# A head's value weights hold its high and low parts side by side: two matmul passes per key tile instead of three, and one VectorE addition per head

## The chip, the core and the metric

One core of a Trainium2 chip runs the whole kernel. The metric is the time of one execution on the device, in microseconds (us), lower is better. The engines are TensorE (PE: matmuls; PEld: its weight loads), VectorE (DVE), ScalarE (ACT), GpSimd (POOL) and SyncE (SP, which here only issues the weight transfers). Each has its own instruction stream; they meet at semaphores.

## What is computed

A two-layer decoder trunk on 512 positions of width 1024, in float32. What matters here are its attention heads of width 64:

```python
# layer B: 12 heads of forgetting attention over the 512 positions (causal)
sc = q @ k.T * scale + logcum_q - logcum_k ; p = softmax(where(mask, sc, -inf)) ; out = p @ v
# layers A and B: 4 heads each of attention into 256 memory tokens
p = softmax(qm @ mk.T * scale) ; out = p @ mv
# then y = concat(mix, mo) @ w_o, layer norms, squared-ReLU MLP
```

Around them stand layer A's gated mixer (a projection, a layer norm, a 128x128 spatial gate), the output projections and the two MLPs.

## The kernel before

Every float32 factor of a matmul is split into a high part (rounded to the reduced float32 type F32R) and a low part (what is left), and a product is three passes: high x high, high x low, low x high. `products` (line 428) issues such passes; nearly all rows of matmuls have its line, L431. `project` (line 439) multiplies a 128-column block of weights by a 128 x 8 x 512 operand: 8 blocks of k, 3 passes each. The weights come by DMA into `w_raw`; ScalarE rounds them to `w_hi` (L844), VectorE subtracts to `w_lo` (L1203, the line of every such subtraction, `rest`), and TensorE waits for that.

Attention goes by steps of two heads (`pair_step`, written out on each engine: lines 551, 916, 1317). Steps 0 and 1 are the memory heads of layer A, 2 (STEP_B) and 9 (STEP_LAST) those of layer B, 3 to 8 the six pairs of fox heads. A step has eight units u, four query blocks for each head. For a unit, TensorE makes the scores (`scores`, bank `sc`), VectorE the row maximum (`row_max`, L1250), ScalarE the exponential (L888), VectorE the normalisation (`normalize`, L1258, tile `probs`), TensorE turns the result (`turn`, L462, bank `tr`), ScalarE takes the high part (`turned_probs`, tiles `pb_hi` for fox, `pa_hi` and `pm_hi` for memory) and VectorE the low part (`pb_lo`, `pa_lo`, `pm_lo`). Then `attend(s, head)` (line 521) multiplies the value weights with them into the bank `pv[head]`. A value tile has 128 columns, 64 of each head of the pair, so that 128 rows come out, of which only the head's own 64 are read. A fox head has four key tiles and sees 512, 384, 256 and 128 queries in them (12 matmuls), a memory head two tiles of 512 (6 matmuls). ScalarE copies the own rows to `mix_hi` (L899) and VectorE subtracts to `mix_lo` (`attended`, line 1266), which raises `mix_ready`.

The order is written by hand. TensorE: for u = 0 to 7 a piece of a projection (`filler(u)`), `turn(u - 2)`, `scores(u)`; then `attend(s, 0)`, `turn(6)`, `filler(8)`, `turn(7)`, `filler(9)`, `attend(s, 1)`, and in steps 2 to 7 `turn_values` (L548), which turns the next pair's values. `attend(s, 1)` waits for the low part of unit 7. VectorE's queue after the last unit: low part of unit 6, `attended(0)`, low part of unit 7, `w_lo` of the next block, a key part, the two `cum_rows` (L1313), `attended(1)`, and the values' low part `v_lo`; then the next step's first `row_max`. Steps 0 to 7 have a projection to put between the units; step 8 and STEP_LAST have only pieces of the output projection (`out_start`), and the last pieces of it need `mix_ready` of the last head. Behind STEP_B, VectorE works on the cumulated gates (`cum`) before `cum_rows`; behind step 1 it begins the spatial gate (L1561).

Of the kernel before, what the change touches and what calls it, by code (L numbers as in the profile page):

```python
# [21 lines left out]
F32 = mybir.dt.float32  # L22
F32R = mybir.dt.float32r

P = 128
HALF = P // 2
# [37 lines left out]
def trunk_kernel(nc, x, mem, a_w_in, a_sgu_ln_g, a_sgu_ln_b, a_w_s, a_b_s, kv_w, kv_b_f, b_w_q,  # L64
# [4 lines left out]
    TT = T // P  # L69
# [40 lines left out]
    with ctx:  # L110
# [3 lines left out]
        def sem(name):  # L114
            return ctx.enter_context(nc.semaphore(name))
# [4 lines left out]
        def put(name, shape, dtype, offset=None):  # L120
            size = 4
            for n in shape[1:]:
                size *= n
            if offset is None:
                offset = base[0]
                base[0] += (size + 63) // 64 * 64
            assert offset + size <= nc.sbuf_usable_end, (name, offset + size)
            return nc.alloc_sbuf_tensor_at(name, shape, dtype, offset=offset)
# [8 lines left out]
        w_raw = put("w_raw", [P, 2, KT, P], F32)  # L137
        mk_twice = put("mk_twice", [P, 2 * MEMPAIRS, M], F32R)
        mk_rest = put("mk_rest", [P, 2 * MEMPAIRS, M], F32R)
        mv_hi = put("mv_hi", [P, MT, MEMPAIRS * P], F32R)  # L140
        mv_lo = put("mv_lo", [P, MT, MEMPAIRS * P], F32R)
        ident = put("ident", [P, P], F32)
        ident_r = put("ident_r", [P, P], F32R)
        ones_r = put("ones_r", [P, P], F32R)
# [51 lines left out]
        qc = put("qc", [P, 2, 2, T], F32R, A0 + 8 * K1)  # L196
        ks = put("ks", [P, 2, 2, T], F32R, A0 + 16 * K1)
        kc = put("kc", [P, 2, 2, T], F32R, A0 + 24 * K1)
        v_hi = put("v_hi", [P, 2, TT, P], F32R, A0 + 32 * K1)
        v_lo = put("v_lo", [P, 2, TT, P], F32R, A0 + 36 * K1)  # L200
        B0 = A0 + 40 * K1

        pb_hi = [put("pb_hi0", [P, TT + 1, T], F32R, B0), put("pb_hi1", [P, TT, TT + 1, P], F32R, B0)]
# [75 lines left out]
        sc_done, max_done, exp_done = sem("sc_done"), sem("max_done"), sem("exp_done")  # L279
        inv_done, probs_ready = sem("inv_done"), sem("probs_ready")  # L280
        pv_done, mix_hi_ready, mix_ready = sem("pv_done"), sem("mix_hi_ready"), sem("mix_ready")
        vt_done, vt_hi, vt_ready = sem("vt_done"), sem("vt_hi"), sem("vt_ready")
        row_ready = sem("row_ready")
        wf_hi_ready, wf_ready = sem("wf_hi_ready"), sem("wf_ready")
# [33 lines left out]
        def fox(s):  # L318
            return STEP_FOX <= s.base < STEP_LAST
# [16 lines left out]
        def other_rows(head):  # L336
            return own_rows(1 - head)
# [89 lines left out]
        def _(pe):  # L427
            def products(target, terms, start=True, stop=True):

                for n, (lhs, rhs) in enumerate(terms):  # L430
                    last = pe.matmul(target, lhs, rhs, start=start and n == 0,  # L431
                                     stop=stop and n == len(terms) - 1)
                return last
# [87 lines left out]
            def attend(s, head):  # L521

                pe.wait_ge(tr_free, tr_index(s, head * TT + TT - 1).at(1))
                wait(pe, mix_ready, s.at(head - 1, 2))
                if s.base == STEP_B and head == 1:
                    pe.wait_ge(f_step, 1)
                c = step_kind(s).slot
                if fox(s) and head == 0:
                    pe.wait_ge(vt_ready, step_kind(s).at(1))
                tiles = TT if fox(s) else MT  # L530
                for j in range(tiles):
                    seen = slice(j * P if fox(s) else 0, T)
                    if fox(s):
                        vh, vl = v_hi[:, c, j], v_lo[:, c, j]
                    else:
                        vh, vl = mv_hi[:, j, c * P:(c + 1) * P], mv_lo[:, j, c * P:(c + 1) * P]
                    ph, pl = seen_places(s, head, j)
                    last = products(pv[head][:, seen], [(vh, ph), (vh, pl), (vl, ph)], j == 0, j == tiles - 1)
                last.then_inc(pv_done, 1)

            def turn_values(s, j):
# [295 lines left out]
        def _(act):  # L837
# [8 lines left out]
            def turned_hi(t, target, source=None):  # L846

                act.wait_ge(tr_done, t.at(1))
                act.copy(target, tr[t.slot][:, :] if source is None else source).then_inc(tr_hi, 1)
# [30 lines left out]
                halves(b, g, [qm[own_rows(head), 2 * c + head, :] for head in range(2)], scale=SCALE)  # L880

            def memory_values(layer):
                turned_hi(Pos(T_MV[layer]), mv_hi[:, :, :], tr[T_MV[layer] % 2][:, :].rearrange("p (m c) -> p m c", m=MT))

            def exponentials(s, u):
                n = keys(s, u) * P
# [29 lines left out]
            def pair_step(s, b=None, g=None, values=None, late=None):  # L916

                mixing = b is not None and s.base < STEP_B
                reading = b is not None and s.base >= STEP_B
                for u in range(8):  # L920
                    if mixing and u in (0, 3, 6):
                        prepare(b.plus(u // 3 + 1))
                    if reading and u in (0, 4, 7):
                        prepare(b.plus((u + 2) // 3 + (u == 0)))
                    if late is not None and u == 1:
                        prepare(late)
                    if u >= 2:
                        turned_probs(s, u - 2)
                    exponentials(s, u)
                    if mixing and u in (2, 5):  # L930
                        step_projection(s, b.plus(u // 3), g.plus(u // 3), u // 3)
                    if reading and u == 2:
                        for head in range(2):
                            fox_head(b, g, 0, head)
                    if reading and u in (5, 6):
                        fox_head(b.plus(1), g.plus(1), 1, u - 5)
                attended(s, 0)
                turned_probs(s, 6)
                turned_probs(s, 7)
                if b is not None:  # L940
                    step_projection(s, b.plus(2), g.plus(2), 2)
                attended(s, 1)
                if values is not None:
                    act.wait_ge(vt_done, values.at(1))
                    act.copy(v_hi[:, values.slot], pv[0][:, :].rearrange("p (t c) -> p t c", t=TT)).then_inc(vt_hi, 1)

            def squares(n, j, g):

# [251 lines left out]
        def _(dve):  # L1200
            def rest(target, whole, hi):

                return dve.tensor_tensor(target, whole, hi.bitcast(F32), ALU.subtract)  # L1203
# [8 lines left out]
            def turned_lo(t, h, target, hi, source=None):  # L1212

                dve.wait_ge(tr_hi, h.at(1))
                rest(target, tr[t.slot][:, :] if source is None else source, hi).then_inc(tr_free, 1)
# [26 lines left out]
                       [qm[own_rows(head), 2 * c + head, :] for head in range(2)], SCALE)  # L1242

            def memory_values(layer):
                turned_lo(Pos(T_MV[layer]), Pos(H_MV[layer]), mv_lo[:, :, :], mv_hi[:, :, :],
                          tr[T_MV[layer] % 2][:, :].rearrange("p (m c) -> p m c", m=MT))

            def row_max(s, u):
                dve.wait_ge(sc_done, s.at(u + 1, 8))
# [16 lines left out]
            def attended(s, head):  # L1266
                rows = slice(head * HALF, (head + 1) * HALF)
                tile = bass.ds(step_tile(s), 1)
                dve.wait_ge(mix_hi_ready, s.at(head + 1, 2))
                rest(mix_lo[rows, tile, :], pv[head][rows, :].rearrange("p (a t) -> p a t", a=1),  # L1270
                     mix_hi[rows, tile, :]).then_inc(mix_ready, 1)

            def gate_stats(n):

# [42 lines left out]
            def pair_step(s, b=None, g=None, values=None, late=None):  # L1317
                mixing = b is not None and s.base < STEP_B
                reading = b is not None and s.base >= STEP_B
                for u in range(8):  # L1320
                    row_max(s, u)
                    if mixing and u in (0, 3, 6):
                        prepare(b.plus(u // 3 + 1))
                    if reading and u in (0, 4):
                        prepare(b.plus(u // 4 + 1))
                    if late is not None and u == 1:
                        prepare(late)
                    if u >= 2:
                        turned_probs(s, u - 2)
                    normalize(s, u)  # L1330
                    if s.base == STEP_A and 1 <= u <= TT:
                        gate_norm(u - 1)
                    if reading and u in (2, 3):
                        fox_query(values, g, u - 2)
                    if reading and u == 6:
                        fox_key(values, g.plus(1), 0)
                turned_probs(s, 6)
                attended(s, 0)
                turned_probs(s, 7)
                if reading:  # L1340
                    prepare(b.plus(3))
                    fox_key(values, g.plus(1), 1)
                if fox(s) and values is not None:
                    cum_rows(values)
                attended(s, 1)
                if values is not None:
                    dve.wait_ge(vt_hi, values.at(1))
                    rest(v_lo[:, values.slot], pv[0][:, :].rearrange("p (t c) -> p t c", t=TT),
                         v_hi[:, values.slot]).then_inc(vt_ready, 1)

            def residual(n, b, g, j, first=True, target=None):

# [447 lines left out]
```

## Time and profile before

| | us |
|---|---|
| median of 3 runs | 1239.83 |
| lowest and highest run | 1237.76, 1242.72 |
| span of the profiled execution | 1237.6 |
| TensorE busy in it | 1162.2 |
| VectorE busy | 649.8 |
| ScalarE busy | 482.1 |

The profile shows one execution; its span runs from the first to the last instruction. Matmuls are pipelined and overlap in the rows, so that their spacing is read from their starts and not from their durations. Some instructions are merged on one row (x2, x12). A bracket such as [0.47 <-ACT mix_hi L899] says how long the engine sat idle before that instruction, and which instruction released it.

### The profile page before, as it was taken

The page shows a single profiled execution, that of the slowest core. Times are in us where ns is not written, and L with a number is a line of the kernel's source. Part 1 is how long each engine was busy: PE and PEld are TensorE (multiplying, and loading weights), DVE is VectorE, ACT ScalarE, POOL GpSimd, SP SyncE. Part 2 cuts the span into 40 slices and gives each one's busy share as a digit, 9 for nine tenths or more (in the row PEclk, how much of TensorE's full clock was granted, in tenths as well). Part 3 has the DMA queues.
Part 4 walks back from the last instruction along what each step waited for, and adds up shares of the span by engine and source line. Part 5 has one row for each costly group of instructions (what it writes and reads, how often), then busy time and mean ns, then how long its engine had stood idle before and what let it go on. Part 6 is the DMA issues. An engine that isn't in the chain of part 4 may idle for free.

```text
span 1237.6 us, 15886 instructions
## 1 busy us (share of the span) xinstructions
PE 1162.2 (94%) x5444; PEld 957.3 (77%) x5444; DVE 649.8 (53%) x1000; ACT 482.1 (39%) x805; POOL 158.5 (13%) x141
## 2 busy tenths in 40 slices
PE   6997989899999999999989999798999999999994
PEld 5776768688888888788668888676788888888883
DVE  4457776654323444343577777667544323544325
ACT  4334633644212334222655556434533222442221
POOL 2204144300000000021501000034200000000002
PEclk9998999899999999999899999998999999999997
DMA  7521132233333333333212121113233333333221
GB/s 215 141 69 51 51 103 83 62 94 102 102 92 95 98 89 102 102 88 92 60 52 69 52 68 52 35 56 98 85 98 90 102 102 87 101 102 101 87 85 68
DMA packets 200714, 107.48 MB, mean 87 GB/s; under 512 B 4512, under 2 KB 197344, under 8 KB 200672
## 3 DMA queue, kind: packets, MB, share of 16 engines
q1 hardware_dynamic: 194304, 99.10, 28.1%
q10 hardware_dynamic: 6368, 7.82, 2.1%
q8 instruction: 26, 0.43, 0.2%
q14 instruction: 16, 0.13, 0.0%
HBM read 104.81 MB, written 2.10 MB: 86 GB/s over the span
## 4 chain that ended last, share of the span: by engine, by line
PE 82%; DVE 10%; ACT 5%; issue 2%; DMA 1%; DVEq 0%; ACTq 0%
PE proj L431 75%; PE pv L431 3%; DVE w_lo L1203 2%; PE tr L462 2%; PE sc L431 2%; ACT w_hi L844 1%; ACT probs L888 1%; DVE probs L1258 1%; DVE neg_max L1250 1%; PE sc L655 1%; DVE mix_lo L1203 1%; DMA w_raw<-in_mem_w_kv 1%; DVE y_nat L1633 0%; DVE z_nat L1288 0%; DVE y_nat L1647 0%
## 5 line engine op out<-in xcount | busy, mean ns | idle before, releaser
L1203 DVE TENSOR_TENSOR w_lo<-w_raw,w_hi 128x1024 fp32r<-128x1024 f32 x186 | 245.7, 1321 | 170.4 <-ACT w_hi L844 167.4
L431 PE MATMUL proj<-x_hi,w_hi 128*128 128x512 f32 x784 | 314.6, 401 | 11.7 <-ACT x_hi L976 6.0
L431 PE MATMUL proj<-x_hi,w_lo 128*128 128x512 f32 x784 | 309.3, 394 | 0.0
L431 PE MATMUL proj<-x_lo,w_hi 128*128 128x512 f32 x784 | 309.0, 394 | 0.0
L844 ACT CAST w_hi<-w_raw 128x1024 fp32r<-128x1024 f32 x186 | 194.3, 1045 | 261.9 <-PE proj L431 259.2
L431 PE MATMUL proj<-h_hi,w_hi 128*128 128x512 f32 x512 | 200.1, 391 | 0.8 <-DVE w_lo L1203 0.8
L431 PE MATMUL proj<-h_hi,w_lo 128*128 128x512 f32 x512 | 199.3, 389 | 0.0
L431 PE MATMUL proj<-h_lo,w_hi 128*128 128x512 f32 x512 | 199.2, 389 | 0.0
L431 PEld LDWEIGHTS proj<-x_hi,w_hi 128*128 128x128 f32 x784 | 149.1, 190 | 45.7 <-ACT x_hi L976 10.4
L431 PEld LDWEIGHTS proj<-x_hi,w_lo 128*128 128x128 f32 x784 | 149.3, 190 | 31.1
L431 PEld LDWEIGHTS proj<-x_lo,w_hi 128*128 128x128 f32 x784 | 149.5, 191 | 29.4 <-POOL x_lo L1668 0.7
L1435 DVE TENSOR_TENSOR h_raw<-relu 128x512 f32<-128x512 f32 x64 | 44.3, 692 | 153.6 <-ACT relu L865 153.6
L865 ACT ACTIVATE relu<-proj 128x512 f32<-128x512 f32 x64 | 38.3, 598 | 192.1 <-PE proj L431 192.1
L431 PEld LDWEIGHTS proj<-h_hi,w_hi 128*128 128x128 f32 x512 | 96.1, 188 | 20.9 <-DVE w_lo L1203 1.2
L431 PEld LDWEIGHTS proj<-h_hi,w_lo 128*128 128x128 f32 x512 | 96.1, 188 | 20.1
L431 PEld LDWEIGHTS proj<-h_lo,w_hi 128*128 128x128 f32 x512 | 96.1, 188 | 19.8
L888 ACT ACTIVATE probs<-sc,neg_max 128x256 f32<-128x256 f32 (+2 forms) x80 | 40.6, 508 | 69.7 <-DVE neg_max L1250 69.6
L431 PE MATMUL proj<-mix_hi,w_hi 128*128 128x512 f32 x128 | 51.9, 405 | 2.9 <-DVE w_lo L1203 1.7
L1668 POOL TENSOR_TENSOR x_lo<-x,x_hi 128x512 fp32r<-128x512 f32 x32 | 43.6, 1373 | 76.0 <-ACT x L972 46.1
L1203 DVE TENSOR_TENSOR h_lo<-h_raw,h_hi 128x512 f32 (+1 forms) x64 | 44.3, 693 | 15.8 <-ACT h_hi L995 15.5
L462 PE MATMUL tr<-ident,probs 128*128 128x128 f32 x184 | 36.3, 292 | 16.1 <-DVE probs L1258 15.7
L431 PE MATMUL proj<-mix_hi,w_lo 128*128 128x512 f32 x128 | 50.5, 394 | 0.0
(223 smaller groups left out, 1292.1 us busy)
## 6 DMA issues: line engine op xcount, KB each, us to landing
w_raw<-in_w_up SPq DMA_DIRECT2D x64, 512.0 KB, 4.1
w_raw<-in_w_down SPq DMA_DIRECT2D x64, 512.0 KB, 3.8
w_raw<-in_w_o SPq DMA_DIRECT2D x16, 512.0 KB, 3.9
w_raw<-in_a_w_in SPq DMA_DIRECT2D x14, 512.0 KB, 3.8
w_raw<-in_kv_w SPq DMA_DIRECT2D x12, 512.0 KB, 3.8
w_raw<-in_mem_w_kv SPq DMA_DIRECT2D x8, 512.0 KB, 5.9
w_raw<-in_b_w_q SPq DMA_DIRECT2D x8, 512.0 KB, 3.8
x_nat<-in_x ACTq DMA_DIRECT2D x2, 1024.0 KB, 12.4
```

The costliest lines, as they stand in the source:

```text
L431: last = pe.matmul(target, lhs, rhs, start=start and n == 0, stop=stop and n == len(terms) - 1)
L462: last = pe.transpose(tr[t.slot][0:n, at:at + rows], piece, ident[0:rows, 0:rows])
L655: last = pe.matmul(bank[:, t:t + 1], part[:, t * P:(t + 1) * P], ones_f[:, 0:1], start=early and t == 0, stop=not early, skip_group_check= ...
L844: act.copy(w_hi[:, b.slot], w_raw[:, b.slot]).then_inc(w_hi_ready, 1)
L865: act.activation(target, proj[g.slot][:, 0:target.shape[-1]], function).then_inc(proj_free[g.slot], 1)
L888: act.activation(probs[:, u % 2, 0:n], sc[u % 2][:, 0:n], ACT.Exp, bias=neg_max[:, u:u + 1], accum_out=row_sum[:, u:u + 1]).then_inc(exp_d ...
L1203: return dve.tensor_tensor(target, whole, hi.bitcast(F32), ALU.subtract)
L1250: dve.tensor_reduce(neg_max[:, u:u + 1], sc[u % 2][:, 0:keys(s, u) * P], AX.X, ALU.max, negate=True).then_inc(max_done, 1)
L1258: dve.tensor_scalar(own, own, inv_sum[:, u:u + 1], None, ALU.mult).then_inc(probs_ready, 1)
L1435: dve.tensor_tensor(raw, wide, wide, ALU.mult).then_inc(relu_sq, 1)
L1668: pool.tensor_tensor(x_lo[:, k], x32[:, k], x_hi[:, k].bitcast(F32), ALU.subtract).then_inc(x_ready, 1)
```

## The change

The value weights of one key tile and one pair become four blocks of 64 columns: head 0's high part, head 0's low part, head 1's low part, head 1's high part. The 128 weights of one head are its two neighbouring blocks. A tile is then two passes, against the high and the low part of the probabilities. The head's own 64 rows of `pv` hold the sum over its high part, the other 64 rows that over its low part (with low x low, which three passes leave out). VectorE forms `mix_lo` as before, waits for it on the new semaphore `mix_part`, and adds the other 64 rows of `pv`; only then is `mix_ready` raised. Where the values are written (once for each layer's memory, once for each pair of fox heads) the instructions are the same in number and size, with targets of 64-element blocks.

```diff
-        mv_hi = put("mv_hi", [P, MT, MEMPAIRS * P], F32R)
-        mv_lo = put("mv_lo", [P, MT, MEMPAIRS * P], F32R)
+        mv_both = put("mv_both", [P, MT * MEMPAIRS, 4, HALF], F32R)
...
-        v_hi = put("v_hi", [P, 2, TT, P], F32R, A0 + 32 * K1)
-        v_lo = put("v_lo", [P, 2, TT, P], F32R, A0 + 36 * K1)
+        v_both = put("v_both", [P, 2, TT, 4, HALF], F32R, A0 + 32 * K1)
...
+        mix_part = sem("mix_part")
...
-                    if fox(s):
-                        vh, vl = v_hi[:, c, j], v_lo[:, c, j]
-                    else:
-                        vh, vl = mv_hi[:, j, c * P:(c + 1) * P], mv_lo[:, j, c * P:(c + 1) * P]
+                    both = v_both[:, c, j] if fox(s) else mv_both[:, j * MEMPAIRS + c]
+                    both = both[:, 2 * head:2 * head + 2, :].rearrange("p q c -> p (q c)")
                     ph, pl = seen_places(s, head, j)
-                    last = products(pv[head][:, seen], [(vh, ph), (vh, pl), (vl, ph)], j == 0, j == tiles - 1)
+                    last = products(pv[head][:, seen], [(both, ph), (both, pl)], j == 0, j == tiles - 1)
...
-                    act.copy(v_hi[:, values.slot], pv[0][:, :].rearrange("p (t c) -> p t c", t=TT)).then_inc(vt_hi, 1)
+                    act.copy(v_both[:, values.slot, :, 0::3, :],
+                             pv[0][:, :].rearrange("p (t h c) -> p t h c", t=TT, h=2)).then_inc(vt_hi, 1)
...
-                rest(mix_lo[rows, tile, :], pv[head][rows, :].rearrange("p (a t) -> p a t", a=1),
-                     mix_hi[rows, tile, :]).then_inc(mix_ready, 1)
+                low = mix_lo[rows, tile, :]
+                rest(low, pv[head][rows, :].rearrange("p (a t) -> p a t", a=1), mix_hi[rows, tile, :]).then_inc(mix_part, 1)
+                dve.wait_ge(mix_part, s.at(head + 1, 2))
+                dve.tensor_tensor(low, low.bitcast(F32), pv[head][other_rows(head), :].rearrange("p (a t) -> p a t", a=1),
+                                  ALU.add).then_inc(mix_ready, 1)
...
-                    rest(v_lo[:, values.slot], pv[0][:, :].rearrange("p (t c) -> p t c", t=TT),
-                         v_hi[:, values.slot]).then_inc(vt_ready, 1)
+                    rest(v_both[:, values.slot, :, 1:3, :], pv[0][:, :].rearrange("p (t h c) -> p t h c", t=TT, h=2),
+                         v_both[:, values.slot, :, 0::3, :]).then_inc(vt_ready, 1)
```

The two functions `memory_values` of ScalarE and VectorE change in the same way as the last hunk.

## Rows read from the trace of the kernel before

**Rows 1.** Page, parts 1 and 4: TensorE busy; chain shares by engine.

```profile
PE 1162.2 (94%) x5444; PEld 957.3 (77%) x5444; DVE 649.8 (53%) x1000; ACT 482.1 (39%) x805; POOL 158.5 (13%) x141
...
PE 82%; DVE 10%; ACT 5%; issue 2%; DMA 1%; DVEq 0%; ACTq 0%
```

**Rows 2.** One fox step by stretch: PE, PEld, DVE, ACT, POOL, clock, DMA.

```profile
689.18:715.60 26.42, 26.42 (x145) 22.52 (x145) 20.37 (x45) 15.29 (x36) 2.45 (x4) 1.00 0.22 60
```

**Rows 3.** Chain in order of time: start, us, what; two attends.

```profile
689.18 1.87 PE pv L431 x12
...
640.44 1.38 PE pv L431 x6
```

**Rows 4.** Groups by shape, VectorE: count | busy us, mean ns | idle.

```profile
L1203 DVE TENSOR_TENSOR mix_lo<-pv,mix_hi 64x512 fp32r<-64x512 f32 x12 | 8.2, 684 | 14.5 <-ACT mix_hi L899 14.5
...
L1203 DVE TENSOR_TENSOR mk_rest<-proj,mk_twice 64x256 fp32r<-64x256 f32 x8 | 3.4, 420 | 2.8 <-ACT mk_twice L859 2.8
...
L1369 DVE SCALAR_TENSOR_TENSOR x<-x,shift 128x512 f32<-128x512 f32 x12 | 16.2, 1350 | 0.0
```

**Rows 5.** Timeline, one fox step: start, us, instruction, [idle before <-releaser].

```profile
718.42 0.49 DVE L1258 TENSOR_SCALAR probs<-probs,inv_sum 128x512 f32<-128x512 f32 x1
...
719.05 0.65 PE L462 MATMUL tr<-ident,probs 128*128 128x128 f32 x4
...
719.53 0.67 DVE L1203 TENSOR_TENSOR mix_lo<-pv,mix_hi 64x512 f32 x1
...
720.35 0.69 DVE L1203 TENSOR_TENSOR pb_lo<-tr,pb_hi 128x512 fp32r<-128x512 f32 x1
...
721.61 0.39 PE L431 MATMUL pv<-pb_hi,v_hi 128*128 128x512 f32 x1
...
724.50 0.70 DVE L1203 TENSOR_TENSOR mix_lo<-pv,mix_hi 64x512 f32 x1 [0.70 <-ACT mix_hi L899]
...
725.22 0.69 DVE L1203 TENSOR_TENSOR v_lo<-pv,v_hi 128x512 fp32r<-128x512 f32 x1
...
728.92 0.42 DVE L1250 TENSOR_REDUCE neg_max<-sc 128x1 f32<-128x256 f32 x1 [0.63 <-PE sc L431]
```

**Rows 6.** Timeline, fox step 7 into step 8.

```profile
777.15 0.69 DVE L1203 TENSOR_TENSOR mix_lo<-pv,mix_hi 64x512 fp32r<-64x512 f32 x1 [0.47 <-ACT mix_hi L899]
...
778.49 0.28 DVE L1250 TENSOR_REDUCE neg_max<-sc 128x1 f32<-128x128 f32 x1
...
779.84 0.33 PE L462 MATMUL tr<-ident,probs 128*128 128x128 f32 x1 [0.80 <-DVE probs L1258]
```

**Rows 7.** Timeline, fox step 8 into the last memory step.

```profile
793.90 0.67 DVE L1203 TENSOR_TENSOR mix_lo<-pv,mix_hi 64x512 fp32r<-64x512 f32 x1
...
795.38 0.50 PE L431 MATMUL pv<-pb_hi,v_hi 128*128 128x512 f32 x1 [0.47 <-DVE pb_lo L1203]
...
800.55 0.44 PE L462 MATMUL tr<-ident,probs 128*128 128x128 f32 x2 [1.60 <-DVE probs L1258]
```

**Rows 8.** Timeline, end of the last memory step.

```profile
811.80 0.67 DVE L1203 TENSOR_TENSOR mix_lo<-pv,mix_hi 64x512 fp32r<-64x512 f32 x1
...
812.40 0.41 DVE L1203 TENSOR_TENSOR pm_lo<-tr,pm_hi 128x256 fp32r<-128x256 f32 x1
...
812.86 0.50 PE L431 MATMUL pv<-pm_hi,mv_hi 128*128 128x512 f32 x1 [1.09 <-DVE pm_lo L1203]
...
815.91 0.50 PE L431 MATMUL proj<-mix_hi,w_hi 128*128 128x512 f32 x1
```

**Rows 9.** Timeline, first memory step of layer B into fox step 3.

```profile
642.46 0.69 DVE L1203 TENSOR_TENSOR mix_lo<-pv,mix_hi 64x512 fp32r<-64x512 f32 x1 [2.48 <-ACT mix_hi L899]
...
646.55 0.30 PE L431 MATMUL sc<-kc,qc 128*128 128x128 f32 x1 [2.25 <-DVE kc L1313]
```

**Rows 10.** Timeline, spatial gate behind the memory steps of layer A.

```profile
147.93 0.36 PE L431 MATMUL sc<-ws_hi,z_hi 128*128 128x256 f32 x1 [0.26 <-DVE gate_even L1561]
```

**Rows 11.** Stretch view, as rows 2, of a slow stretch.

```profile
781.50:785.60 4.10, 4.09 (x15) 3.46 (x16) 2.65 (x8) 1.55 (x4) 0.00 (x0) 0.58 0.44 128
```

More of the change, by code:

```diff
@@ L882, in memory_values @@
             def memory_values(layer):
-                turned_hi(Pos(T_MV[layer]), mv_hi[:, :, :], tr[T_MV[layer] % 2][:, :].rearrange("p (m c) -> p m c", m=MT))
+                turned_hi(Pos(T_MV[layer]), mv_both[:, :, 0::3, :],
+                          tr[T_MV[layer] % 2][:, :].rearrange("p (m h c) -> p m h c", h=2, c=HALF))
             def exponentials(s, u):
@@ L1244, in memory_values @@
             def memory_values(layer):
-                turned_lo(Pos(T_MV[layer]), Pos(H_MV[layer]), mv_lo[:, :, :], mv_hi[:, :, :],
-                          tr[T_MV[layer] % 2][:, :].rearrange("p (m c) -> p m c", m=MT))
+                turned_lo(Pos(T_MV[layer]), Pos(H_MV[layer]), mv_both[:, :, 1:3, :], mv_both[:, :, 0::3, :],
+                          tr[T_MV[layer] % 2][:, :].rearrange("p (m h c) -> p m h c", h=2, c=HALF))
             def row_max(s, u):
```

## The prediction

> **What bounds the kernel now.** I read the page first. TensorE is busy for 1162.2 of 1237.6 us, and the chain that ended last is TensorE's for 82% and VectorE's for 10% [rows 1]. So a matmul taken out is worth its price, but only where TensorE is what ends last, and the shares don't say where that is. Next the stretches, for one step of fox attention with a projection in it: TensorE is busy in all of the 26.42 us, VectorE in 20.37 of them [rows 2]. Such a step looks TensorE-bound with room on VectorE. Then the timeline of that step, because the room has to be where the new work falls; the reader is to see there how close the low part of unit 7 comes before `attend(s, 1)` [rows 5]. Last, the places behind the steps where a bracket shows TensorE idle until VectorE: 0.80 us at the start of step 8, 0.47 and 1.60 around its second attend, 1.09 in the last memory step, 2.25 behind STEP_B, 0.26 in the spatial gate [rows 6 to 10]. At these VectorE is the path, and a longer VectorE queue is paid in full.
>
> **What is removed.** Four matmuls of twelve for each of 12 fox heads, two of six for each of 8 memory heads. Twelve take 1.87 us and six take 1.38 [rows 3]; as each pass has the same columns, a third is 0.62 and 0.46. In all 12 x 0.62 + 8 x 0.46 = 11.1 us of TensorE, 0.9% of the span. That is the most that the change can give.
>
> The six memory matmuls stand 0.23 us apart [rows 3]. The Trainium skill (TensorE: Matmul & The Clock Gate, Back-to-back issue gap) gives about 131 ns per matmul of 512 columns for a sustained stream, and 81 ns at 128. By that a memory head would save 0.26 and a fox head some 0.4, and the sum below would end about 1.8 us higher; the trace doesn't agree with it, and its spacing is used.
>
> **What is added.** One VectorE instruction for each of 20 heads, 64x512, from SBUF and PSUM, behind a wait for the one before it. The trace has no such addition across the row halves. The nearest row is the subtraction it follows, of the same shape and with one operand in PSUM: 684 ns, 0.69 us rounded up. The bounds are 420 ns, half the columns, and 1350 ns, the dearest 512-column instruction with two tensors [rows 4]; it can't be free, since it reads every column. I take 0.69, the same shape. Around it come gaps. `v_lo`, after a subtraction on the other row half, starts 0.02 after that one's end (724.50 + 0.70, then 725.22) [rows 5], whereas `pm_lo`, on the same rows as the instruction before it, starts 0.07 before that one's end (811.80 + 0.67, then 812.40) [rows 8]. The addition waits for its input, so I put 0.03 ahead of it; it reads the other half, so I put 0.03 behind it too.
>
> With a head 1 the gap behind exists already, and the queue grows by 0.69 + 0.03 = 0.72. With a head 0 the subtraction starts at t, the addition at t + 0.70, the next instruction at t + 1.42.
>
> The Trainium skill (VectorE: DVE Perf Modes, Two Vector instructions with no wait between them) says that an instruction whose PSUM input begins in another quarter of the partitions than the last PSUM input is held until all before it have finished. The two gaps above agree with it. Without the hold the instruction behind a head 0 would start 0.10 earlier, and the sum would end some 0.6 lower, at no change.
>
> Storing the values in 64-element blocks I cost at nothing: same count, same size, 0.69 us for `v_lo` [rows 5], with the bounds 0 and one more such 0.69 in each of six steps; the next reader of them is an attend most of a step away. Loads aren't touched, and their issue only moves with `w_lo`.
>
> **Where it falls, step by step.**
>
> Fox steps 3 to 6, head 0. TensorE would finish `attend(s, 0)` 0.62 earlier. But `turn(7)` starts at 719.05 and needs `probs` of unit 7, which ends at 718.42 + 0.49 = 718.91 and comes from a chain of maximum and exponential that doesn't contain the attend [rows 5]. All but 0.1 us becomes a wait. Behind it, VectorE: `mix_lo` at 719.53, addition until 719.53 + 1.39, `pb_lo` of unit 7 at 720.95 instead of 720.35, ready at 721.64; with 0.05 to TensorE, as in [rows 7], `attend(s, 1)` starts at 721.69 instead of 721.61 [rows 5]. Head 0 brings a loss of 0.08.
>
> Head 1. The attend itself is 0.62 shorter. `w_lo`, the key part and `cum_rows` come 0.60 later than before, and what took up 0.70 of idle before `mix_lo` takes that up now [rows 5]. The addition then pushes the next `row_max` by 0.72; against TensorE that is about 0.6 late, and before the `row_max` after that one (unit 1) VectorE sat idle for 0.63 [rows 5]: it is absorbed there. TensorE, which has projection pieces until then, keeps its 0.62. A step nets -0.62 + 0.08 = -0.54, four steps -2.16.
>
> Step 7 into 8. Step 8 has no projection, and TensorE sits idle until its first `probs` [rows 6], so VectorE's queue counts: +0.60 from head 0, less the 0.47 that it sat idle before `mix_lo` [rows 6], +0.72: +0.85. The attend's 0.62 hides nothing.
>
> Step 8 into the last. The low part of unit 7 ends the wait of `attend(s, 1)`: it started so that the attend came 1.48 after `mix_lo`'s start [rows 7]; now it is 1.42 + 0.69 + 0.05 = 2.16, +0.68. The attend gives back 0.62. The addition of head 1 is before the next step's first `row_max`, for which TensorE sits idle for 1.60 [rows 7]: +0.72. Together +0.78.
>
> Last memory step. Head 0: `pm_lo` starts at 811.80 + 1.42 = 813.22 instead of 812.40, +0.82, and the attend waits for it [rows 8]. The attend gives back 0.46, the addition of the last head puts +0.72 before the output projection at 815.91 [rows 8]: +1.08.
>
> STEP_B. Head 0 is hidden behind the idle 2.48 before `mix_lo` [rows 9]. Behind head 1, VectorE leads to the scores for which TensorE is idle [rows 9]: -0.46 + 0.72 = +0.26.
>
> Layer A, steps 0 and 1. Both second attends shorten the way (-0.92), the head 0s again wait for `probs`, and the last addition stands before the spatial gate, where TensorE waits for VectorE [rows 10]: -0.92 + 0.72 = -0.20.
>
> Sum: -0.20 + 0.26 - 2.16 + 0.85 + 0.78 + 1.08 = +0.61 us. The span of 1237.6 becomes 1238.2; that execution's span is 2.2 under the median of the runs, so the median goes from 1239.83 to 1240.4.
>
> **The rivals.**
>
> Both attends count (0.13). If `probs` of unit 7 isn't what holds `turn(7)`, because the maximum before it moves up too, steps 3 to 6 win 0.54 more each: -1.6 in all, 1238.3. Against it stand the 0.14 us between `probs` and the turn [rows 5].
>
> VectorE hides everything (0.05). Of 26.42 us it is idle for 6 [rows 2]; if all additions fell into such room, the whole 11.1 would stay: 1228.7. Against it are the idle brackets in rows 6 to 10.
>
> A dearer addition (0.09), the slower side. At 1.35 us [rows 4] each of the additions on the path costs 0.66 more: one in each of steps 3 to 6, two each in 7, 8 and the last, one each in STEP_B and layer A, 12 in all, 7.9 us: 1248.3. Steps 3 to 6 decide: from 0.69 + 0.54 = 1.23 us on they lose instead of winning. For it speaks that both halves are read at once, against it that all 64x512 rows with a PSUM operand are near 0.68.
>
> The clock (0.14). In the stretch behind the 0.80 idle, the granted clock was 0.58 for 4.1 us [rows 11], mostly the lower level of 1.2 GHz, and TensorE had been waiting repeatedly before it. This costs 4.1 x 0.42 = 1.7 us where TensorE is the path. Longer waits in steps 7, 8 and the last could add two such stretches: 1243.8. The Trainium skill (TensorE: Matmul & The Clock Gate, The HAM clock gate) says the same of idle time: too much of it halves the clock.
>
> The third pass wasn't worth its share (0.03). If weights of neighbouring passes load slower, or each matmul takes longer, and no attend shortens, the nine attends whose saving is in the sum lose it: the second ones of steps 3 to 6 and 8, and those of steps 0, 1, 2 and the last, 5 x 0.62 + 4 x 0.46 = 4.9: 1245.3.
>
> **How the numbers follow.** My forecast has 0.56. A measurement of this kernel can tell about 0.5% from no change, that is 6.2 us. Faster by more is one rival, 0.05; slower by more is the dear addition, 0.09; all others are within, 0.86. The range goes from 1238.3 less half the runs' own spread of 5, 1235.8, to the two slow stretches plus the same, 1246.3; 0.14 lie outside.
>
> **What would show it.** Eight `pv` rows for a fox head, about 1.25 us; four for a memory head, 0.92. Twenty new VectorE rows of 64x512 near 0.69. In steps 3 to 6, TensorE idle for some 0.5 us before the turn of unit 7 and 0.1 before `attend(s, 1)`, and a step of 25.9 us instead of 26.42. The waits at rows 6 to 8 longer, by 0.8, 0.8 and 1.1 in their sums. The prediction is wrong if steps 3 to 6 keep 26.4 us or fall to 25.2, or if the addition isn't near 0.7 us.

## The result, and the profile after

| | before | after |
|---|---|---|
| median of the first runs (6 each) | 1239.27 | 1242.76 |
| median beside it, later (27 and 10 runs) | 1239.33 | 1243.32 |
| span of the profiled execution | 1237.6 | 1240.7 |
| TensorE busy | 1162.2 | 1151.5 |
| VectorE busy | 649.8 | 663.0 |

The ratio is 1.0026 (95% interval 1.0014 to 1.0038), and 1.0032 (1.0021 to 1.0043) the second time: slower by 3.5 and 4.0 us, within the 0.5% that I called no change, but not the +0.6 that I forecast. The working, then, is some 3 us off, and a little under half of that lies in one term.

The page of the changed kernel, parts 1 and 4, which answers to [rows 1]:

```profile
PE 1151.5 (93%) x5380; PEld 943.1 (76%) x5380; DVE 663.0 (53%) x1020; ACT 482.0 (39%) x805; POOL 158.8 (13%) x141
...
PE 78%; DVE 12%; ACT 6%; issue 2%; DMA 1%; ACTq 0%; DVEq 0%
```

TensorE lost 64 matmuls and 10.7 us, VectorE got 20 instructions and 13.2 us. Of the chain that ended last, TensorE has 4 points less and VectorE 2 more. The added instruction in the groups by shape (count | busy us, mean ns | idle):

```profile
L1272 DVE TENSOR_TENSOR mix_lo<-mix_lo,pv 64x512 fp32r<-64x512 f32 x12 | 8.2, 686 | 0.4
L1272 DVE TENSOR_TENSOR mix_lo<-mix_lo,pv 64x512 f32 x8 | 5.5, 686 | 0.3
```

686 ns, as taken. So the price was right, and the question is where it lies. The timeline of the fox step that answers to [rows 5]:

```profile
719.34 0.49 DVE L1257 TENSOR_SCALAR probs<-probs,inv_sum 128x512 f32<-128x512 f32 x1
719.96 0.65 PE L461 MATMUL tr<-ident,probs 128*128 128x128 f32 x4 [0.48 <-DVE probs L1257]
720.45 0.67 DVE L1202 TENSOR_TENSOR mix_lo<-pv,mix_hi 64x512 f32 x1
721.16 0.69 DVE L1272 TENSOR_TENSOR mix_lo<-mix_lo,pv 64x512 f32 x1
721.88 0.69 DVE L1202 TENSOR_TENSOR pb_lo<-tr,pb_hi 128x512 fp32r<-128x512 f32 x1
722.30 0.39 PE L430 MATMUL proj<-x_hi,w_lo 128*128 128x512 f32 x1
722.49 1.22 DVE L1202 TENSOR_TENSOR w_lo<-w_raw,w_hi 128x1024 fp32r<-128x1024 f32 x1
722.70 0.49 PE L430 MATMUL pv<-pb_hi,v_both 128*128 128x512 f32 x1
723.03 0.40 PE L430 MATMUL pv<-pb_lo,v_both 128*128 128x512 f32 x1
...
723.73 0.69 DVE L1202 TENSOR_TENSOR kc<-proj,ks 64x512 fp32r<-64x512 f32 x1
...
724.02 0.62 PE L545 MATMUL pv<-ident,v_tmp 128*128 128x128 f32 x4
...
724.57 0.47 PE L430 MATMUL proj<-x_hi,w_hi 128*128 128x512 f32 x1
```

As foretold, TensorE waits 0.48 for the turn of unit 7, the subtraction, the addition and `pb_lo` follow each other 0.71 and 0.72 apart, and `attend(s, 1)` waits a little (matmuls of 512 columns stand 0.23 apart, so that 722.53 would have been its time, and it started at 722.70). What I had not looked for are the two places behind that: the first two matmuls of the attend are 0.33 apart, 0.10 more than in a stream, which I call the restart below, and from the transposes of the next values at 724.02 to the next projection it takes 0.55.

The waits of TensorE that answer to [rows 6 to 9], and the output projection:

```profile
646.29 0.30 PE L430 MATMUL sc<-kc,qc 128*128 128x128 f32 x1 [2.94 <-DVE kc L1315]
...
781.31 0.33 PE L461 MATMUL tr<-ident,probs 128*128 128x128 f32 x1 [1.46 <-DVE probs L1257]
...
797.44 0.49 PE L430 MATMUL pv<-pb_hi,v_both 128*128 128x512 f32 x1 [1.16 <-DVE pb_lo L1202]
...
802.68 0.44 PE L461 MATMUL tr<-ident,probs 128*128 128x128 f32 x2 [2.32 <-DVE probs L1257]
...
816.07 0.50 PE L430 MATMUL pv<-pm_hi,mv_both 128*128 128x512 f32 x1 [1.94 <-DVE pm_lo L1202]
...
819.38 0.50 PE L430 MATMUL proj<-mix_hi,w_hi 128*128 128x512 f32 x1 [0.73 <-DVE mix_lo L1272]
```

The first five were 2.25, 0.80, 0.47, 1.60 and 1.09 before; at the output projection there was no bracket.

To compare kernels I use three distances between starts of attends, from the same timelines: A, in microseconds like the others, is one period of steps 3 to 6 (a quarter of the way from the first `pv` matmul of `attend(3, 1)` to that of `attend(7, 1)`), B goes from there to `attend(8, 1)`, C from there to the last step's second attend. The last column is the mean granted clock over the runs of the kernel. One run of e4 was in a slow state (1592.46 us at a granted clock of 0.692) and is left out of its row.

| kernel | median, us | ratio to before (95%) | A | B | C | clock |
|---|---|---|---|---|---|---|
| before | 1239.3 | 1 | 26.45 | 20.89 | 17.48 | 0.977 |
| before again, one trace | | | 26.45 | 20.17 | 17.31 | |
| changed | 1242.76 | 1.0026 (1.0014, 1.0038) | 26.25 | 22.26 | 18.63 | 0.975 |
| changed again (e11) | 1243.32 | 1.0032 (1.0021, 1.0043) | 26.26 | 22.33 | 18.60 | 0.974 |
| no addition (e1) | 1234.45 | 0.9965 (0.9952, 0.9978) | 25.81 | 19.97 | 16.67 | 0.976 |
| addition only (e2) | 1245.79 | 1.0047 (1.0034, 1.0060) | 26.74 | 23.06 | 18.86 | 0.976 |
| fox heads only (e3) | 1240.35 | 1.0007 (0.9998, 1.0016) | 26.27 | 22.06 | 17.65 | 0.976 |
| memory heads only (e4) | 1241.39 | 1.0021 (1.0012, 1.0030) | 26.46 | 20.85 | 18.21 | 0.974 |
| head 0's addition behind pb_lo (e5) | 1241.60 | 1.0015 (1.0006, 1.0025) | 26.35 | 22.20 | 17.66 | 0.975 |
| head 0's addition off VectorE (e6) | 1241.42 | 1.0018 (1.0009, 1.0027) | 26.47 | 21.84 | 17.88 | 0.974 |
| most additions off the path (e7) | 1238.30 | 0.9993 (0.9983, 1.0002) | 26.45 | 20.27 | 16.67 | 0.977 |
| e6, bank freed earlier (e9) | 1238.14 | 0.9996 (0.9987, 1.0005) | 25.79 | 21.84 | 17.87 | 0.975 |
| e7, bank freed earlier (e10) | 1236.42 | 0.9978 (0.9969, 0.9987) | 25.80 | 20.89 | 16.68 | 0.975 |

### The profile page after: what moved, and what is told of

Same layout as the page of the kernel before. It is cut to its first block, busy times and chain, and to the rows that moved or that the text cites. A ratio compares the mean times of both kernels' runs of the same rounds, so it can differ in the third digit from the quotient of the medians.

```text
span 1240.7 us, 15778 instructions
## 1 busy us (share of the span) xinstructions
PE 1151.5 (93%) x5380; PEld 943.1 (76%) x5380; DVE 663.0 (53%) x1020; ACT 482.0 (39%) x805; POOL 158.8 (13%) x141
## 4 chain that ended last, share of the span: by engine, by line
PE 78%; DVE 12%; ACT 6%; issue 2%; DMA 1%; ACTq 0%; DVEq 0%
PE proj L430 73%; DVE w_lo L1202 3%; PE tr L461 2%; ACT w_hi L841 2%; PE sc L430 1%; PE pv L430 1%; ACT probs L886 1%; DVE neg_max L1249 1%; DVE probs L1257 1%; DVE mix_lo L1202 1%; PE sc L652 1%; DMA w_raw<-in_mem_w_kv 1%; DVE y_nat L1635 0%; DVE z_nat L1290 0%; DVE inv_sum L1255 0%
## 5 line engine op out<-in xcount | busy, mean ns | idle before, releaser
L461 PEld LDWEIGHTS tr<-ident,probs 128*128 128x128 f32 x184 | 23.5, 147 | 39.9 <-DVE probs L1257 30.1
```

The lines of the kernel that those rows point to most:

```text
L461: last = pe.transpose(tr[t.slot][0:n, at:at + rows], piece, ident[0:rows, 0:rows])
```

## The experiments

After the result I held that both halves of the sum were real (passes worth their price, additions paid where VectorE leads), that a step from 3 to 6 wins only 0.2 us, and that a stretch at the low clock behind STEP_B (granted clock 0.66 in 646 to 651 us), which the first trace of before doesn't have, came from the longer wait there.

**No addition, and addition only.** The two parts of the change, each alone:

```diff
# e1: the changed kernel
-                rest(low, ...).then_inc(mix_part, 1)
-                dve.wait_ge(mix_part, s.at(head + 1, 2))
-                dve.tensor_tensor(low, low.bitcast(F32), pv[head][other_rows(head), :]..., ALU.add).then_inc(mix_ready, 1)
+                rest(low, ...).then_inc(mix_ready, 1)
# e2: the kernel before, three passes
-                rest(mix_lo[rows, tile, :], ...).then_inc(mix_ready, 1)
+                (the subtraction, the wait and the addition of the changed kernel)
```

> The changed kernel without the addition: two passes for each key tile, and the mixture's low part is ready after the subtraction alone. What the values' low part contributes is left out of the mixture. Theory (the passes are worth their price, and the addition on VectorE's path takes it back): -0.92 in layer A, -0.46 behind the first memory step of layer B and the clock full there, -0.62 to -0.72 in each of the fox steps 3 to 6 (the second attend no longer waits), 0 in step 7, -0.62 in step 8, -0.46 in the last step: together 5.1 to 5.5 us faster than before, some 8.7 faster than the changed kernel. Rival (the third pass wasn't worth its share, or the new layout costs what it gives): within 1 us of before. Rival (VectorE's placement plays no part, only the addition's own time where TensorE ends last): 11 us faster than before.

> The kernel before, with its three passes, and the added VectorE instruction for each head (what it adds is the other head's rows, so the mixture is not the right one; only its time is asked for). Theory: about +0.15 in each of steps 3 to 6, +1.2 in step 7, +1.4 in step 8, +1.4 in the last step, +0.7 in STEP_B, +0.7 before the spatial gate: +6 us, and +7.6 if the longer wait behind STEP_B again brings a stretch at the low clock. Rival (the addition hides in VectorE's room): within 1 us. Rival (the loss is the new layout's or the second matmul's, not the addition's): +3.5 or less.

Measured: 4.9 us faster, and 6.4 slower. A period of steps 3 to 6 falls to 25.81, 0.64 under before: the pass is worth the 0.62 I took from [rows 3], and only the second attend's, since the first attend's is eaten by the wait for the turn. So neither "the third pass wasn't worth its share" nor "everything hides" holds. In e2 A grows by 0.29 where I expected 0.15. The same stretch of e1, beside the changed kernel's above:

```profile
717.20 0.65 PE L460 MATMUL tr<-ident,probs 128*128 128x128 f32 x4 [0.47 <-DVE probs L1256]
...
718.50 0.69 DVE L1201 TENSOR_TENSOR pb_lo<-tr,pb_hi 128x512 fp32r<-128x512 f32 x1
...
719.77 0.39 PE L429 MATMUL pv<-pb_hi,v_both 128*128 128x512 f32 x1
720.00 0.39 PE L429 MATMUL pv<-pb_lo,v_both 128*128 128x512 f32 x1
...
720.36 0.69 DVE L1201 TENSOR_TENSOR kc<-proj,ks 64x512 fp32r<-64x512 f32 x1
...
720.98 0.62 PE L544 MATMUL pv<-ident,v_tmp 128*128 128x128 f32 x4
...
721.36 0.48 PE L429 MATMUL proj<-x_hi,w_hi 128*128 128x512 f32 x1
```

From the turn of unit 7 to the attend it takes 2.57 instead of 2.74 (0.17), the first two matmuls of the attend are 0.23 apart instead of 0.33 (0.10), and from the transposes to the projection it takes 0.38 instead of 0.55 (0.17). Together 0.44, which is the whole difference in A (26.25 less 25.81). The last of the three is a bank: the projection writes where the key part was, and `kc` frees it; in the changed kernel `kc` ends at 723.73 + 0.69 = 724.42, 0.15 before the projection starts, in e1 at 721.05, when TensorE is still in the transposes. In e2 the attend is 0.62 longer, so `kc` is in time again (0.38 from the transposes to the projection in all four steps), and what is left is 0.17 + 0.10 = 0.27, against 0.29 measured.

**Fox heads only, memory heads only.** The heads that don't change take three passes from the new layout:

```diff
-                    last = products(pv[head][:, seen], [(both, ph), (both, pl)], j == 0, j == tiles - 1)
+                    terms = [(both, ph), (both, pl)]
+                    if three_passes(s):          # e3: the memory heads, e4: the fox heads
+                        terms.append((blocks[:, 1:3, :].rearrange("p q c -> p (q c)"), ph))
+                    last = products(pv[head][:, seen], terms, j == 0, j == tiles - 1)
```

> The change for the 12 fox heads alone; the memory heads take three passes from the new layout (the third with the two middle blocks, so that the own rows get all of it) and have no addition. By the forecast's terms: -2.16 in steps 3 to 6, +0.85 and +0.78 behind them, so -0.5 against before. By the trace of the changed kernel, in which a step from 3 to 6 won only some 0.2: -0.8 + 0.9 + 0.7 = +0.8. In both, the wait behind STEP_B is as before and the clock stays full behind it. Rival (the slow clock behind STEP_B is chance and not the longer wait): it is there in this kernel too, and the time is about +2.4.

> The change for the 8 memory heads alone; the fox heads take three passes from the new layout and have no addition. By the forecast's terms: -0.20 in layer A, +0.26 in STEP_B, +1.08 in the last step: +1.1 us against before. With a stretch at the low clock behind STEP_B, whose wait is again 2.9 us: +2.7, and matmuls 0.42 us apart there instead of 0.23. Rival (the slow clock there is chance): +1.1, and 0.23 apart.

Measured: +1.0 and +2.0 by the medians. The ratios, 1.0007 and 1.0021, add up to 1.0028; the changed kernel's is 1.0026. e3 has A and nearly all of B, e4 has the last step's part of C and nothing of A. For the fox heads +0.8 was right and my forecast of -0.5 wrong. The clock part of e3's expectation fell, since its clock doesn't stay full behind STEP_B, and with it the cause that I had given for e4's. In the view by stretches (PE, PEld, DVE, ACT, POOL, clock, DMA), 646 to 651 us of the first trace of before, of e3, whose wait behind STEP_B is 2.25 us, and of the changed kernel, whose wait is 2.94:

```profile
646.00:651.00 5.00, 4.45 (x23) 3.79 (x24) 2.85 (x8) 1.02 (x4) 0.00 (x0) 1.00 0.22 64
```

```profile
646.00:651.00 5.00, 5.00 (x21) 4.12 (x20) 1.73 (x7) 0.83 (x3) 0.00 (x0) 0.74 0.38 107
```

```profile
646.00:651.00 5.00, 4.71 (x17) 3.92 (x18) 1.94 (x6) 0.46 (x2) 0.00 (x0) 0.66 0.24 73
```

**Before again.** I took another trace of before for that:

> The kernel before once more, for its trace behind STEP_B, where TensorE waits for 2.25 us. Theory (the slow clock there in the changed kernel came from the longer wait of 2.94): full clock in 646 to 651 us again. Rival (chance, or any wait there suffices; kernels with a wait of 2.25 had it too): granted clock near 0.7 in that stretch.

The low clock is there, too, behind a wait of 2.22 us:

```profile
646.00:651.00 5.00, 4.70 (x17) 3.98 (x18) 2.27 (x6) 0.46 (x2) 0.00 (x0) 0.67 0.26 68
```

A later kernel (e9 below) waits for 2.94 us there and has the full clock behind it:

```profile
646.94 0.30 PE L435 MATMUL sc<-kc,qc 128*128 128x128 f32 x1 [2.94 <-DVE kc L1342]
```

```profile
646.00:651.00 5.00, 4.06 (x21) 3.51 (x22) 2.90 (x7) 1.02 (x4) 0.00 (x0) 1.00 0.11 29
```

The longer wait isn't the cause; the first trace of before was the exception. This one is at full clock in step 8 instead, where the first had the slow stretch of [rows 11], and its B is 0.7 shorter for it; behind STEP_B it is the other way round, and from `attend(2, 1)` to `attend(3, 1)` it takes 30.01 instead of 28.39. Such a stretch comes and goes between traces of one kernel, and a difference of 1 to 2 us between two single traces can be that alone.

**Head 0's addition behind `pb_lo`.** If the 0.44 is what VectorE has to do before the projection, and not the wait of the attend, then another order on VectorE can't win it:

```diff
                 attended(s, 0)          # now the subtraction alone
                 turned_probs(s, 7)
+                added(s, 0)             # the addition
                 if reading:
                     prepare(b.plus(3))
```

> The changed kernel with head 0's addition moved on VectorE from in front of the low part of unit 7 to right behind it; head 1's stays. Theory (in steps 3 to 6 head 0's addition costs through all that VectorE has to do before TensorE's next projection, whose bank the key part frees, and not through attend(s, 1) alone): attend(s, 1) no longer waits, but the projection behind it waits longer instead, so that a step from 3 to 6 keeps its 26.2 us; 0.7 us is won at the second attend of step 8 and 0.7 to 0.85 at that of the last step. In all 1.5 us faster than the changed kernel, some 2 slower than before. Rival (the wait of attend(s, 1) and its restart are the whole cost): steps 3 to 6 at 25.9 us, 2.5 faster than the changed kernel.

```profile
721.28 0.39 PE L430 MATMUL pv<-pb_hi,v_both 128*128 128x512 f32 x1
721.36 1.22 DVE L1202 TENSOR_TENSOR w_lo<-w_raw,w_hi 128x1024 fp32r<-128x1024 f32 x1
721.51 0.39 PE L430 MATMUL pv<-pb_lo,v_both 128*128 128x512 f32 x1
...
722.61 0.69 DVE L1202 TENSOR_TENSOR kc<-proj,ks 64x512 fp32r<-64x512 f32 x1
...
723.45 0.47 PE L430 MATMUL proj<-x_hi,w_hi 128*128 128x512 f32 x1 [0.33 <-DVE kc L1202]
```

The attend doesn't wait and doesn't restart, and TensorE waits for `kc` instead, 0.33 by the bracket. In the changed kernel and in e5 the projection starts 0.15 behind the end of `kc` in three of the steps 3 to 6 and 0.05 behind it in the other; in before, e1 and e2, which don't wait there, it is 0.30 or more. A is 26.35, not the rival's 25.9 and even 0.1 above the changed kernel. C is 0.97 shorter than the changed kernel's, as there the low part was last. B stays: the second attend of step 8 comes 0.69 earlier behind the first, but from `attend(7, 1)` to there it takes 0.63 longer. Of this 0.21 is VectorE's queue, which stands that much later behind the attend (0.16 of it is the attend's own earlier start), and 0.42 is the first projection piece of step 8, which starts within a stretch at the low clock in e5 (1.44 from its start to the transposes, its first matmul 0.80 long) and ahead of one in the changed kernel (1.02 and 0.50). So the second part is the clock's, and B says nothing against the 0.7 expected at step 8. The time is 1.2 us under the changed kernel's first median and 1.7 under its second; 1.5 was expected.

**Off VectorE.** GpSimd is idle at this point of a step. The Trainium skill (PSUM — Partial Sum Buffer, The four PSUM rules) says that GpSimd has no access to PSUM; no run here shows it. So ScalarE, idle behind `pb_hi` of unit 7, copies the other 64 rows into SBUF, and GpSimd adds them. In e6, whose edit is shown, head 0 of steps 3 to 9 goes this way. In e7 both fox heads do, and three memory heads take three passes instead of an addition:

```diff
+            def spilling(s, head):          # ScalarE, 0.58 us; head 0: behind turned_probs(s, 7)
+                act.copy(spill[own, :, :], pv[head][other_rows(head), :]...).then_inc(spilled, 1)
...
+            def added(s, head):             # GpSimd
+                pool.wait_ge(mix_part, 2 * s + head + 1)
+                pool.wait_ge(spilled, s - STEP_FOX + 1)
+                pool.tensor_tensor(low, low.bitcast(F32), spill[own, :, :], ALU.add).then_inc(mix_ready, 1)
```

> The changed kernel with head 0's addition of steps 3 to 9 taken off VectorE: ScalarE copies the other 64 rows of the bank into SBUF behind the high part of unit 7, and GpSimd, idle there, adds them. Head 1's additions stay on VectorE. Theory (head 0's addition costs 0.43 in a step from 3 to 6, head 1's nothing): a step from 3 to 6 takes 25.8 us, 1.7 less in four; steps 7, 8 and the last win 0.7 each: 3.8 faster than the changed kernel, some 0.3 faster than before. Rival (head 1's addition is what costs in steps 3 to 6): they keep 26.2 us. Rival (GpSimd's addition slows VectorE beside it): neighbouring VectorE instructions longer than in the changed kernel, and less than 3 us won.

> As the last kernel, with both heads' additions of the fox steps and that of the last step's head 0 on ScalarE and GpSimd; the second heads of the second, third and last memory step take three passes (the third with the two middle blocks) and need no addition; the other three additions stay on VectorE. Theory: -0.46 in layer A, 0 behind STEP_B, -2.5 in steps 3 to 6, -0.9 to -1.2 in steps 7 and 8, 0 to -0.5 in the last: 3.9 to 4.7 us faster than before. Rival (ScalarE's copies are on its own path to the next exponential): no more than the kernel before it.

Both missed: e6 is 1.3 us under the changed kernel's first median instead of 3.8, e7 0.8 under before instead of 3.9 to 4.7. C fell as expected, A went up to 26.47 and 26.45, which is before's. From e7:

```profile
720.73 2.21 POOL L1801 TENSOR_TENSOR mix_lo<-mix_lo,spill 64x512 fp32r<-64x512 f32 x1 [4.32 <-ACT spill L909]
...
722.46 1.27 DVE L1339 TENSOR_SCALAR kc<-cum,head_rows 64x512 fp32r<-64x512 f32 x2
...
723.00 0.66 PE L553 MATMUL pv<-ident,v_tmp 128*128 128x128 f32 x4 [0.38 <-POOL mix_lo L1801]
```

GpSimd's addition took 2.21 us, and the transposes of the next values waited for it, because they waited for `mix_ready`. They overwrite the bank, which GpSimd never reads. So in e9 (and likewise in e10) they wait for the two that do read it:

```diff
                 if s is not None:
-                    pe.wait_ge(mix_ready, s.at(1, 2))
+                    pe.wait_ge(spilled, s.at(1 - STEP_FOX))
+                    pe.wait_ge(mix_part, s.at(1, 2))
```

> The kernel with head 0's addition on ScalarE and GpSimd, but the transposes of the next values wait for ScalarE's copy and VectorE's subtraction, the only two that read the bank, instead of for GpSimd's addition, which read 2.21 us long beside VectorE's w_lo and held those transposes back to 1.75 behind the start of attend(s, 1) instead of 1.22. Theory (in steps 3 to 6 head 0's addition costs 0.43 and head 1's nothing): a step falls from 26.5 to 25.9 us, so 2.4 us less in four steps and 0.5 in step 7: 1238.5, 0.7 faster than before. Rival (head 1's addition has a cost there too): 26.1 or more a step.

> The kernel with the additions off the path, with the same mended wait for the transposes of the next values. Theory: a step from 3 to 6 at 25.9 us; 2.4 us less in four steps and 0.5 in step 7 than its forerunner's 1238.3: 1235.4, 3.8 us faster than before. Rival (GpSimd's additions, which made the key rows of VectorE beside them 0.60 instead of 0.48 us long, cost as much somewhere else): 1237 or more.

> The changed kernel once more, beside the two above and before on the same chip. Theory (terms read from the trace: -0.1 in layer A, +0.3 in STEP_B, -0.8 in steps 3 to 6, +2.9 behind them, together +2.2, and the rest of the 3.5 measured is the clock's): +2 to +4 us against before, and again 26.2 us for each step from 3 to 6. Rival (the first measurement was far off by chance): within 1 us of before.

A fell to 25.79 and 25.80. In e9 head 1's addition is still on VectorE, and A is that of e1, which has none: **head 1's addition costs nothing in steps 3 to 6, head 0's costs all of the 0.44.** e9 came out at 1238.14 (1238.5 expected), though the 0.5 expected in step 7 doesn't show: B is 21.84 in both, at a granted clock of 0.92 in e6's trace and 0.84 in e9's. e10, at 1236.42, is the fastest kernel that leaves nothing out: 2.9 us under before, with an interval wholly below 1, and 6.9 under the changed kernel beside it. It is 1.0 above what I expected, and below the 1237 of the rival. A part of that can be seen in its step 7:

```profile
774.50 1.27 DVE L1342 TENSOR_SCALAR kc<-cum,head_rows 64x512 fp32r<-64x512 f32 x2
...
776.13 0.30 PE L435 MATMUL sc<-kc,qc 128*128 128x128 f32 x1 [0.32 <-DVE kc L1342]
```

The two rows of `cum_rows` take 1.27 beside GpSimd instead of 0.97 in the changed kernel, and in step 7, without filler, TensorE waits for them. Its B is 0.9 longer than e1's: 0.3 of that is this, and 0.5 the first projection piece of step 8, which runs at the low clock for the most part here and at full clock in e1.

## Why the prediction was right or wrong

**The range and the sign.** The median lies in the range, within the 0.5% that I called the same, and on the slower side of my 1240.4. The direction came from the right picture: some 11 us of TensorE taken out, and more than that given back through 20 additions of 0.69 and the waits around them. That the median lies in the range is owed to the range's width of 10.5 us as much as to the sum, which is 3 us short.

**What is removed and added.** Right. Eight `pv` matmuls of a fox head take 1.22 us where I wrote 1.25, and the addition 686 ns. The new layout costs nothing that shows: the subtraction that writes the values' low part takes 0.69 in `v_both` as it did in `v_lo`, and e1, which has the layout, gains 0.64 a period where the pass alone was put at 0.62. The lower bound, the dearer addition of 1.35 and the rival "the third pass wasn't worth its share" are out.

**The turn of unit 7.** Right: 0.48 of idle before it, and in e1 0.47. The first attend's saving is gone in every kernel measured, so the rival "both attends count" is out.

**Steps 3 to 6.** This step failed. I wrote -0.54 a step and -2.16 in all; measured is -0.20 a step (26.45 to 26.25) and -0.8 in all, nearer to the 26.4 that I had named as a sign of being wrong than to the 25.9 forecast. The loss through head 0 that I put at 0.08 is 0.44 in three pieces. The start of the attend: 0.16 against before instead of 0.08. `pb_lo` starts 5.51 behind the first attend, as I had worked it out (715.44 to 720.95; now 716.37 to 721.88), but from its end to the attend it takes 0.13, where I took 0.05 from [rows 7]. The restart: 0.10, which I left out, though [rows 7] has the duration 0.50 for an attend's first matmul after a wait, against 0.39 in [rows 5]. And the bank: 0.17, which is my own instruction not followed. I wrote that `w_lo`, the key part and `cum_rows` come 0.60 later and that this takes up 0.70 of idle before `mix_lo`. It does, but I asked only who waits at the end of that queue and not who waits for each instruction in it; `kc` frees the bank of the next projection, and once the attend is 0.62 shorter it has 0.3 us to spare. Head 1's 0 was right.

**Step 7 to the last.** Right to 0.2 us in the two first traces. From `mix_hi` of step 7 to the output projection I had 0.85 + 0.78 + 1.08 = 2.71; the rows moved from +0.54 at `attend(7, 0)` (768.38 to 768.92) to +3.47 at the output projection (815.91 to 819.38), which is 2.93. The granted clock over this way is 0.93 in both, so like is compared with like; the second trace of before has 1.00 there and takes 46.65 instead of 47.53. I said that the brackets of rows 6 to 8 would grow by 0.8, 0.8 and 1.1; they grew by 0.66, 1.41 and 0.85. That was loosely put. A bracket behind a shortened attend grows by what the attend saved as well: the two in step 8 by 1.41, less 0.62 for the attend, is 0.79 of path. In the last step 0.85, with the 0.73 that now stands before the output projection and less the attend's 0.46, is 1.12.

**STEP_B and layer A.** Right where the trace lets one read it. From `attend(2, 1)` at 640.28 to the scores at 646.55 it took 6.27, now 6.54 (639.75 to 646.29): +0.27 for +0.26. In layer A the way between the second attends of steps 0 and 1 shortens by 0.47, and that from the latter to the spatial gate grows by 0.31: -0.16 for -0.20.

**The sum.** With the measured terms it is -0.2 + 0.3 - 0.8 + 2.9 = +2.2 instead of +0.6, and the runs say 3.5 and 4.0, with 1.7 at the lower end of the first interval and 2.6 at that of the second. **What is left, over a microsecond, isn't settled.** The mean granted clock is 0.975 and 0.974 over the changed kernel's runs, against 0.977 over before's. If every low stretch fell where TensorE is the path, a fall of 0.002 to 0.003 over 1240 us would be 2.5 to 3.7 us, by estimate. Before's own runs give less. Of the 77 taken beside the experiments, the 15 with a granted clock of 0.971 to 0.974 have a mean of 1240.8 us and a mean clock of 0.973, the other 62 have 1238.8 and 0.978: 2.0 us for 0.006, so 0.7 to 1.0 for this fall, again an estimate. The memory heads alone have the lower clock as well (0.974, +2.0 where their terms give 1.2), the fox heads alone hardly (0.976, +1.0 where theirs give 0.8). So my rival, the clock, may be a part of what is left; it isn't shown to be, and not where I put it. The clock over the way from `attend(7, 0)` to the output projection is the same 0.93 in the first traces of before and of the changed kernel and 0.91 in the changed kernel's second, in which that way is as long as in its first (50.50 and 50.46), and the stretch behind STEP_B, for which I took it at first, was there in before as well.

## What to carry to other kernels

When an instruction is put into a queue, follow each instruction behind it to the one who waits for it, and take the smallest slack of them all: a bank that one of them frees can have less than the end of the queue. An instruction that ends a wait late costs the restart besides, here 0.10 us for a matmul. When a buffer's last reader changes, look again at what its next writer waits for; waiting for the result instead of the last read cost 0.65 us a step here.

## What was not expected of the hardware

GpSimd and VectorE, side by side in SBUF, slowed each other down, and in these traces it was the one that started second that took longer. From e10:

```profile
721.08 1.22 DVE L1221 TENSOR_TENSOR w_lo<-w_raw,w_hi 128x1024 fp32r<-128x1024 f32 x1
721.22 2.21 POOL L1804 TENSOR_TENSOR mix_lo<-mix_lo,spill 64x512 fp32r<-64x512 f32 x1 [4.31 <-ACT spill L912]
...
725.20 1.30 POOL L1804 TENSOR_TENSOR mix_lo<-mix_lo,spill 64x512 fp32r<-64x512 f32 x1 [1.77 <-ACT spill L912]
...
726.16 1.42 DVE L1221 TENSOR_TENSOR w_lo<-w_raw,w_hi 128x1024 fp32r<-128x1024 f32 x1
```

GpSimd's addition of 64x512 took 2.21 us where VectorE's `w_lo` was already running, which kept its 1.22. Where GpSimd was first it took 1.30, and the `w_lo` that started in its last 0.3 us took 1.39 to 1.42. With no VectorE instruction beside it the addition took 1.27 to 1.29. Of the two `cum_rows`, the one that starts beside GpSimd's addition went from 0.48 to 0.78 us and the other kept its 0.48, and `kc`, with one operand in PSUM, kept its 685 ns. The Trainium skill (GPSIMD Engine Reference, Specifications) says that GpSimd shares its SBUF interfaces with VectorE and contends with instructions in a two-port mode or with two inputs from SBUF. The trace agrees for `w_lo`, which has two inputs in SBUF, and for `kc`, which by the subtraction hasn't; `cum_rows` has one, and no row shows in which mode it ran.

The granted clock's slow stretches aren't tied to one place of the program. Of the thirteen traces, all but the first of before and that of e9, whose wait is one of the longest, have one behind STEP_B (granted clock 0.66 to 0.82 in 646 to 651 us), and all but the second of before have one in step 8 (0.84 to 0.92 over B, and 1.00 in that one).
